# Reading the moving columns of two matrix products in other orders (one-core transformer kernel, Trainium2)

## The chip, the core and the metric

The kernel runs on one core of one Trainium2 chip. The metric is the device time of one execution in microseconds. TensorE has two clock levels, 1.2 and 2.4 GHz; the profile gives the granted clock as a share of the higher one. At 2.4 GHz one column takes 0.4167 ns.

## What is computed

The reference runs two transformer blocks on 256 tokens of width 2048 in fp32. The first is a hybrid of stick-breaking attention and multi-scale pooling, the second retention, a gated delta rule, cross attention and a feed-forward layer. The change touches only the feed-forward layer at the end:

```
h = rms_norm(x, norm_ffn_g)                                # (256, 2048)
x = x + square(relu(h @ w_ff1)) @ w_ff2                    # w_ff1 (2048, 8192), w_ff2 (8192, 2048)
return rms_norm(x, norm_final_g)
```

## The kernel before, in words

**Precision.** Each fp32 operand of a large product is split into a rounded high part and the rest, the low part, both held as fp32r. A product is high times high, plus high times low, plus low times high, summed in PSUM. The matmul takes one operand as stationary weights (128 by 128) and streams the other, the moving operand, past it column by column; each moving column gives one output column in PSUM.

**Weights.** All large weight matrices come in 471 units of up to 2048 columns by 128 partitions. SyncE loads a unit from HBM (`raw`), ScalarE writes the high part (`whi`, line 1704), VectorE subtracts to get the low part (`wlo`, line 2042), each in two halves; `raw`, `whi` and `wlo` have three buffers each. TensorE takes the units in the order of `pairs()`. The order of all engines is written out by hand in `make_plan`, and each engine runs its own steps of that list.

**The feed-forward layer.** It runs in eight blocks of 1024 hidden features. A block b has four products `f1` (256 hidden features each) and then four products `f2` (512 output columns each), each of two units.

- `f1` (kind "T"): the weights are stationary, the activations `AA` moving. `AA` holds the high parts of all activations and, 4352 columns further on, the low parts. For each of 16 pieces of 128 input features and each of 2 output halves there are two matmuls: `whi` against high and low activations together (512 columns, an access of two runs of 256, into one PSUM bank), and `wlo` against the high activations alone (256 columns, into the bank's first half). So a block has 128 matmuls of 512 columns and 128 of 256. VectorE later adds the two halves of the bank (`summed`, line 2065), which reads PSUM with alternating elements 256 columns (1 KB) apart.
- `f2` (kind "N"): the activations `BB` (the block's hidden features) are stationary, the weights moving. For each of 8 pieces and 2 token halves there are three matmuls of 512 columns into one PSUM bank: `whi`, `wlo`, `whi`. So a block has 4 products x 16 x 3 = 192 matmuls of 512 columns. VectorE adds the bank to the residual `XT`.

PSUM has two accumulators of two banks (`double0`, `double1`) that the products use in turn, so reading one out lies beside the next product. Every matmul is issued by `mm_group` (line 1346); all 512 columns of an operand are read in ascending order, `out` in the same order.

**Elsewhere in the kernel**, and of use below: in the gated delta rule the matmuls `g_up` (out `bank`, moving `TT`, stationary `Mn`, 64 columns) read the moving operand by `odd(TT_..., d)`, that is in runs of d columns with d columns left out between them, for d = 2, 4, 8, 16, 32 in this order; `g_down` (moving `Cm`, stationary `Tn`) reads 64 adjacent columns. These are in full fp32, for which the trace has two matmul records each.

Of the kernel before, what the change touches and what calls it, by code (L numbers as in the profile page):

```python
# [13 lines left out]
T = 256  # L14
# [1060 lines left out]
def program(nc, A):  # L1075
# [4 lines left out]
    def S(name):  # L1080
        if name not in sems:
            sems[name] = nc.alloc_semaphore("s_" + name)
        return sems[name]
# [36 lines left out]
    for i in range(4):  # L1120
        o = ar.off
# [139 lines left out]
    def two(x):  # L1261
        return x.rearrange("p (a b) -> p a b", a=2)
# [48 lines left out]
    def hi_of(j):  # L1311
        o = set_off(j)[0]
        return whi[j % SPL][:, o:o + UNIT]

    def lo_of(j):
        o = set_off(j)[1]
        return wlo[j % SPL][:, o:o + UNIT]
# [14 lines left out]
    gdn_end = at["g_tr", 7]["m"]  # L1332


    def tensor_program(q):
        asked = {}

        def free(f):
            if f:
                q.wait_ge(S(f[0]), f[1])  # L1340
# [4 lines left out]
        def mm_group(out, lhsT, rhs, start=True, stop=True):  # L1345
            return q.matmul(out, lhsT, rhs, start=start, stop=stop, skip_group_check=True)  # L1346
# [4 lines left out]
        def operand(pr, a):  # L1351

            if pr["ready"][0] == "b_lo":
                return BB[:, :, a * T:(a + 1) * T]
            if pr["kind"] == "W":
                o, n = a * L, L
            elif pr["tag"] in ("gp", "q", "mp", "ga", "ma"):
                o, n = a * L + META, T
            else:
                o, n = a * T, T  # L1360
            return AA[:, :, o:o + n]

        def mm(key):
            j, half = key
            pi, k, kt, nc_ = units[j]
            pr = P.pairs[pi]
            kind, out = pr["kind"], double[pr["bank"]]
            if k == 0 and half == 0:
                free(pr["freed"])
            if j < 2:  # L1370
                q.wait_ge(S("first_lo"), 2 * j + half + 1)
            else:
                q.wait_ge(S("w_lo"), 2 * j + half + 1)
            split = j in P.split
            if split:
                q.wait_ge(S("w_lo"), 2 * j + 2)
            wh = hi_of(j)[:, 0:kt * nc_].rearrange("p (t c) -> p t c", t=kt)
            wl = lo_of(j)[:, 0:kt * nc_].rearrange("p (t c) -> p t c", t=kt)
            for i in range(kt) if split else range(half * kt // 2, (half + 1) * kt // 2):
                a = k * kt + i  # L1380
                name, ready = pr["ready"]
                if j < 2 and i % 4 == 2:
                    q.wait_ge(S("w_lo"), 2 * j + half + 1)
                if asked.get(name, 0) < ready[a]:
                    asked[name] = ready[a]
                    q.wait_ge(S(name), ready[a])
                both = operand(pr, a)
                hh, hl = both[:, 0, :], both[:, 1, :]
                first, last = k == 0 and i == 0, k == pr["nu"] - 1 and i == kt - 1
                for m in (half,) if split else range(1 if kind == "G" else 2):  # L1390
                    cs = slice(m * 128, (m + 1) * 128)
                    if kind == "W":
                        o = out[:, m * 512:m * 512 + L]
                        mm_group(o, wh[:, i, cs], hh, start=first, stop=False)
                        mm_group(o, wh[:, i, cs], hl, start=False, stop=False)
                        ins = mm_group(o, wl[:, i, cs], hh, start=False, stop=last)
                    elif kind == "N":
                        o = out[:, m * 512:(m + 1) * 512]
                        mm_group(o, hh[:, cs], wh[:, i, :], start=first, stop=False)
                        mm_group(o, hh[:, cs], wl[:, i, :], start=False, stop=False)  # L1400
                        ins = mm_group(o, hl[:, cs], wh[:, i, :], start=False, stop=last)
                    else:
                        n, c = (nc_, slice(0, nc_)) if kind == "G" else (128, cs)
                        mm_group(out[0:n, m * 512:m * 512 + 2 * T], wh[:, i, c], both, start=first, stop=False)
                        ins = mm_group(out[0:n, m * 512:m * 512 + T], wl[:, i, c], hh, start=False, stop=last)
            if split and k:
                ins.then_inc(S("last"), 1)
            elif half == 1:
                ins.then_inc(S("w_used"), 1)
# [276 lines left out]
        for stage, key in P.steps:  # L1686
            if stage == "mm":
                mm(key)
            elif stage in own:
                own[stage](key, at[stage, key])  # L1690
# [1195 lines left out]
    with nc.Block() as block:  # L2886
        @block.tensor
        def _(q):
            tensor_program(q)

        @block.scalar
        def _(q):
            scalar_program(q)

        @block.vector
        def _(q):
            vector_program(q)

        @block.gpsimd
        def _(q):  # L2900
            gpsimd_program(q)

        @block.sync
        def _(q):
            sync_program(q)
# [55 lines left out]
```

## Time and profile before

| | us |
|---|---|
| median of 2 runs | 2870.13 (2869.91 to 2870.35) |
| profiled execution, span from first to last instruction | 2866.7 |
| feed-forward products in the profile | 2187 to 2857 |
| TensorE busy | 2829.8 (99%) |
| VectorE busy | 1931.7 (67%) |
| ScalarE busy | 1355.2 (47%) |

The page has one time for the profiled execution, its span; the runs lie 3.4 us above it. "PE" rows are matmuls, "PEld" rows weight loads, which overlap them. A row of the timeline gives start, duration, and a count if several alike follow each other; the distance between the starts of two matmuls is what one costs in the stream, its duration also holds the way through the array. In names such as `double<-AA,whi` the first input is the moving operand and the second the stationary one.

### The profile page before, as it was taken

How to read it: one execution, taken by the hardware profiler on the slowest of the kernel's cores; microseconds unless marked ns; L12 is line 12 of the kernel's file. 1: busy time of each engine (PE TensorE's matmuls, PEld its weight loads, DVE VectorE, ACT ScalarE, POOL GpSimd, SP SyncE). 2: the span in 40 equal slices, each digit the busy share in tenths (PEclk: the TensorE clock that was granted, in tenths of full speed). 3: DMA queues.
4: the chain of work that ended last, by engine and by line, in shares of the span. 5: the costliest groups of instructions: out<-in, count | busy, mean ns of one | idle time of the engine just before them, and what ended most of it. 6: DMA issues, size and time to landing. Idle time of an engine off the chain costs nothing.

```text
span 2866.7 us, 38752 instructions
## 1 busy us (share of the span) xinstructions
PE 2829.8 (99%) x15872; PEld 2442.7 (85%) x15872; DVE 1931.7 (67%) x2513; ACT 1355.2 (47%) x1729; POOL 57.2 (2%) x102
## 2 busy tenths in 40 slices
PE   9999999999999999999999999999999999999998
PEld 8899888888888888888888888888888888888887
DVE  7645557678766658888888875456666655566556
ACT  5433654357443446555555543444345434444434
POOL 0000210000000000000000000000000000000000
PEclk9999999999999999999999999999999999999999
DMA  7444444564555544334343455544354454554453
GB/s 278 183 184 162 143 166 185 197 231 177 197 184 193 204 151 162 141 139 147 133 145 123 145 175 192 187 182 162 146 200 182 178 204 182 200 200 182 186 196 147
DMA packets 72849, 506.66 MB, mean 177 GB/s; under 512 B 8384, under 2 KB 8512, under 8 KB 12896
## 3 DMA queue, kind: packets, MB, share of 16 engines
q1 hardware_dynamic: 71136, 497.83, 46.9%
q0 software_dynamic: 1104, 5.90, 0.6%
q8 instruction: 126, 2.06, 0.3%
q10 hardware_dynamic: 432, 0.45, 0.0%
q14 instruction: 51, 0.42, 0.0%
HBM read 499.95 MB, written 2.10 MB: 175 GB/s over the span
## 4 chain that ended last, share of the span: by engine, by line
PE 86%; DVE 9%; ACT 3%; issue 2%; DMA 1%; SPq 0%; DVEq 0%; POOL 0%; ACTq 0%
PE double L1346 80%; PE bank L1346 5%; DVE cacc L2048 2%; DVE wlo L2042 2%; ACT whi L1704 1%; DVE cst L2065 1%; PE bank L1349 1%; DVE cacc L2045 1%; ACT L1900 0%; DVE Tn L2556 0%; DVE cst L2042 0%; DVE Cm L2042 0%; ACT tmp L1905 0%; DMA vec<-in_vec 0%; DMA raw<-in_wall 0%
## 5 line engine op out<-in xcount | busy, mean ns | idle before, releaser
L1346 PE MATMUL double<-AA,whi 128*128 128x512 f32 (+1 forms) x5008 | 1643.1, 380 | 3.5 <-DVE wlo L2042 3.3
L1346 PE MATMUL double<-AA,wlo 128*128 128x256 f32 (+1 forms) x4624 | 1297.0, 281 | 0.0
L1704 ACT ACTIVATE whi<-raw 128x1024 fp32r<-128x1024 f32 x926 | 925.2, 1049 | 780.3 <-PE double L1346 748.5
L2042 DVE TENSOR_TENSOR wlo<-raw,whi 128x1024 fp32r<-128x1024 f32 (+1 forms) x934 | 1101.7, 1214 | 229.9 <-ACT whi L1704 227.6
L1346 PEld LDWEIGHTS double<-AA,whi 128*128 128x128 f32 x5008 | 915.9, 188 | 181.2 <-DVE wlo L2042 5.2
L1346 PEld LDWEIGHTS double<-AA,wlo 128*128 128x128 f32 x4624 | 874.7, 189 | 1.5
L1346 PE MATMUL double<-whi,AA 128*128 128x512 f32 x1536 | 487.9, 393 | 0.5 <-DVE wlo L2042 0.5
L1346 PEld LDWEIGHTS double<-whi,AA 128*128 128x128 f32 x1536 | 288.5, 188 | 61.0 <-DVE wlo L2042 1.3
L1346 PE MATMUL double<-whi,BB 128*128 128x512 f32 x1024 | 316.8, 389 | 0.0
L1346 PE MATMUL double<-wlo,AA 128*128 128x512 f32 x768 | 299.1, 389 | 0.0
L1346 PEld LDWEIGHTS double<-whi,BB 128*128 128x128 f32 x1024 | 192.2, 188 | 40.1
L1346 PE MATMUL double<-wlo,BB 128*128 128x512 f32 x512 | 199.3, 389 | 0.0
L1346 PEld LDWEIGHTS double<-wlo,AA 128*128 128x128 f32 x768 | 144.4, 188 | 28.7
L2065 DVE TENSOR_REDUCE tmp<-double 128x512 f32<-128x1024 f32 x60 | 73.4, 1224 | 133.1 <-PE double L1346 133.1
L1346 PEld LDWEIGHTS double<-wlo,BB 128*128 128x128 f32 x512 | 96.1, 188 | 19.8
L2042 DVE TENSOR_TENSOR XT<-double,XT 128x512 f32<-128x512 f32 x64 | 41.3, 686 | 93.0 <-PE double L1346 93.0
L1980 ACT ACTIVATE tmp<-tmp 128x512 f32<-128x512 f32 x32 | 20.2, 633 | 172.1 <-DVE tmp L2048 172.1
L1346 PE MATMUL double<-BB,whi 128*128 128x512 f32 x256 | 90.0, 394 | 0.0
L2048 DVE SCALAR_TENSOR_TENSOR cacc<-cst,vec,cacc 128x256 f32<-128x256 f32 x144 | 69.8, 485 | 5.1
L1346 PE MATMUL double<-BB,wlo 128*128 128x256 f32 x256 | 71.6, 280 | 0.0
L2042 DVE TENSOR_TENSOR X<-double,X 128x512 f32<-128x512 f32 x48 | 33.2, 691 | 53.4 <-PE double L1346 52.5
L2042 DVE TENSOR_TENSOR BB<-tmp,BB 128x512 fp32r<-128x512 f32 x40 | 27.7, 693 | 49.5 <-ACT BB L1753 49.5
(335 smaller groups left out, 1722.2 us busy)
## 6 DMA issues: line engine op xcount, KB each, us to landing
raw<-in_wall SPq DMA_DIRECT2D x462, 1024.0 KB, 4.8
raw<-in_wall SPq DMA_DIRECT2D x9, 256.0 KB, 6.7
X<-in_xT SPq DMA_DIRECT2D x1, 2048.0 KB, 11.4
Mm<-in_memT POOLq DMA_DIRECT2D x1, 2048.0 KB, 15.5
tmp<-rqk POOLq DMA_DIRECT2D x16, 128.0 KB, 2.2
mblk<-in_memT SPq DMA_DIRECT2D x8, 256.0 KB, 4.5
dec<-in_dec POOLq DMA_DIRECT2D x1, 1536.0 KB, 8.6
hs<-in_hsT SPq DMA_DIRECT2D x4, 272.0 KB, 5.2
```

What stands on the lines that cost most here:

```text
L1346: return q.matmul(out, lhsT, rhs, start=start, stop=stop, skip_group_check=True)
L1349: return q.transpose(out, in_, C("ident") if ident is None else ident)
L1704: q.activation(hi_of(j)[:, c], raw[j % RAW][:, c], ACT.Copy).then_inc(S("w_hi"), 1)
L1980: q.activation(x, x, ACT.Square).then_inc(S("f_act"), 1)
L2042: return q.tensor_tensor(out, a, b, o)
L2045: return q.tensor_scalar(out, a, s, None, o)
L2048: return q.scalar_tensor_tensor(out=out, in0=a, scalar=s, in1=b, op0=o0, op1=o1)
L2065: q.reduce_sum(out, both, mybir.AxisListType.X).then_inc(S("sum"), 1)
```

## The change

A table `WAYS` gives thirteen of the sixteen half-blocks another order in which moving columns are read, with the output columns permuted in the same way, so each output column gets what it got before. `("turn", r)` goes in turns between the two halves of the 512 columns, r columns of the one and then r of the other. `("leap", s, r)` reads every s-th chunk of r columns, then the next set, s sets in all. In `f1` a "turn" applies to the 512-column matmuls only (`walk2`), a "leap" to the 256-column ones only (`walk`). In `f2` both apply to all three matmuls. Block 0 of `f1` and blocks 6 and 7 of `f2` stay as they are.

```diff
+    WAYS = {("f1", 1): ("turn", 16), ("f1", 2): ("turn", 4), ("f1", 3): ("turn", 2), ("f1", 4): ("leap", 2, 16), ("f1", 5): ("leap", 4, 16),
+            ("f1", 6): ("leap", 16, 2), ("f1", 7): ("turn", 64),
+            ("f2", 0): ("leap", 2, 16), ("f2", 1): ("leap", 4, 16), ("f2", 2): ("leap", 8, 2), ("f2", 3): ("leap", 2, 8),
+            ("f2", 4): ("turn", 16), ("f2", 5): ("turn", 2)}
...
+        def walk(pr, x):
+
+            way = WAYS.get((pr["tag"], pr["idx"][0])) if pr["tag"] in ("f1", "f2") else None
+            if way is None or way[0] == "turn" and pr["tag"] == "f1":
+                return x
+            if way[0] == "leap":
+                return x.rearrange("p (b s r) -> p s b r", s=way[1], r=way[2])
+            return x.rearrange("p (a b r) -> p b a r", a=2, r=way[1])
+
+        def walk2(pr, x):
+
+            way = WAYS.get((pr["tag"], pr["idx"][0])) if pr["tag"] == "f1" else None
+            if way is None or way[0] == "leap":
+                return x
+            return x.rearrange("p a (b r) -> p b a r", r=way[1])
...
-                        o = out[:, m * 512:(m + 1) * 512]
-                        mm_group(o, hh[:, cs], wh[:, i, :], start=first, stop=False)
-                        mm_group(o, hh[:, cs], wl[:, i, :], start=False, stop=False)
-                        ins = mm_group(o, hl[:, cs], wh[:, i, :], start=False, stop=last)
+                        o, h_, l_ = [walk(pr, x) for x in (out[:, m * 512:(m + 1) * 512], wh[:, i, :], wl[:, i, :])]
+                        mm_group(o, hh[:, cs], h_, start=first, stop=False)
+                        mm_group(o, hh[:, cs], l_, start=False, stop=False)
+                        ins = mm_group(o, hl[:, cs], h_, start=False, stop=last)
...
-                        mm_group(out[0:n, m * 512:m * 512 + 2 * T], wh[:, i, c], both, start=first, stop=False)
-                        ins = mm_group(out[0:n, m * 512:m * 512 + T], wl[:, i, c], hh, start=False, stop=last)
+                        o = out[0:n, m * 512:m * 512 + 2 * T]
+                        if pr["tag"] == "f1" and WAYS.get(("f1", pr["idx"][0]), ("",))[0] == "turn":
+                            mm_group(walk2(pr, two(o)), wh[:, i, c], walk2(pr, both), start=first, stop=False)
+                        else:
+                            mm_group(o, wh[:, i, c], both, start=first, stop=False)
+                        ins = mm_group(walk(pr, o[:, 0:T]), wl[:, i, c], walk(pr, hh), start=False, stop=last)
```

## Rows read from the trace of the kernel before

**Rows 1.** The page: span, busy time of each engine, granted clock by slices.

```profile
span 2866.7 us, 38752 instructions
PE 2829.8 (99%) x15872; PEld 2442.7 (85%) x15872; DVE 1931.7 (67%) x2513; ACT 1355.2 (47%) x1729; POOL 57.2 (2%) x102
PEclk9999999999999999999999999999999999999999
```

**Rows 2.** The chain that ended last, 2180 to 2867 (start us, us, what).

```profile
2187.15 670.27 PE double L1346 x3392
```

**Rows 3.** Who waited for whom, 2190 to 2857 (us in total, times, longest us).

```profile
ACT whi L1704 <- PE double L1346: 200.9, 86, 3.7
DVE XT L2042 <- PE double L1346: 90.4, 32, 3.2
DVE tmp L2065 <- PE double L1346: 79.3, 29, 3.3
```

**Rows 4.** Busy time in two stretches: block 1's f1, then its f2.

```profile
2241.44:2285.81 44.37, 44.37 (x257) 39.23 (x256) 27.38 (x27) 19.55 (x22) 0.00 (x0) 1.00 0.47 179
2285.81:2329.38 43.57, 43.57 (x194) 36.04 (x193) 24.90 (x25) 17.23 (x18) 0.00 (x0) 1.00 0.53 204
```

**Rows 5.** Timeline of TensorE within an f1 product (two runs of 256, then 256).

```profile
2354.91 0.39 PE L1346 MATMUL double<-AA,whi 128*128 128x512 f32 x1
2355.14 0.28 PE L1346 MATMUL double<-AA,wlo 128*128 128x256 f32 x1
...
2357.34 0.39 PE L1346 MATMUL double<-AA,whi 128*128 128x512 f32 x1
```

**Rows 6.** Timeline within an f2 product (512 adjacent columns each).

```profile
2309.66 0.62 PE L1346 MATMUL double<-whi,BB 128*128 128x512 f32 x2
2310.11 0.39 PE L1346 MATMUL double<-wlo,BB 128*128 128x512 f32 x1
...
2312.38 0.39 PE L1346 MATMUL double<-whi,BB 128*128 128x512 f32 x1
```

**Rows 7.** Timeline, one head pair: d = 2, adjacent columns, d = 32.

```profile
1131.69 0.68 PE L1346 MATMUL bank<-TT,Mn 128*64 128x64 f32 x8
1136.18 0.68 PE L1346 MATMUL bank<-Cm,Tn 128*64 128x64 f32 x8
1162.12 0.68 PE L1346 MATMUL bank<-TT,Mn 128*64 128x64 f32 x8
```

**Rows 8.** The chain, 1967 to 1971: full-fp32 matmuls of 256 columns in cross attention.

```profile
1967.07 3.46 PE bank L1346 x16
```

**Rows 9.** All groups of VectorE: two ways of reading PSUM.

```profile
L2065 DVE TENSOR_REDUCE tmp<-double 128x512 f32<-128x1024 f32 x60 | 73.4, 1224 | 133.1 <-PE double L1346 133.1
L2042 DVE TENSOR_TENSOR X<-double,X 128x512 f32<-128x512 f32 x48 | 33.2, 691 | 53.4 <-PE double L1346 52.5
```

## The prediction, made before the kernel was run

> **What bounds the kernel now.** I read the page first. TensorE is busy in 99% of the span, VectorE in 67%, ScalarE in 47%, and all forty slices stand at the higher clock level [rows 1]. Then the chain that ended last: it runs through 3392 matmuls in one piece of 670.27 us, nearly the whole feed-forward layer, which is where all of the change lies; the reader is to see that no other engine's work stands between them [rows 2]. The waits say the same from the other side: ScalarE and VectorE wait for TensorE, up to 3.7 us at a time, and TensorE is in no line of them [rows 3]. In two stretches of one block TensorE is busy all of the time, VectorE for 27.4 of 44.4 us and 24.9 of 43.6 us, and the transfers take half of the DMA engines [rows 4]. So here a nanosecond on a matmul of the stream is a nanosecond on the kernel, up or down: a slower TensorE only makes the others wait more, and a faster one has 16 us a block in hand before VectorE would bind.
>
> Within the stream, a 512-column matmul over adjacent columns costs (2312.38 - 2309.66) / 12 = 226.7 ns [rows 6]. A pair of `f1` costs (2357.34 - 2354.91) / 7 = 347 ns, of which about 230 are the 512 columns in two runs and 117 the 256 columns [rows 5]. As a check, 128 x 347 ns = 44.4 us and 192 x 226.7 ns = 43.5 us, as the two stretches have it [rows 4]. At 2.4 GHz 512 columns are 213.3 ns and 256 are 106.7: the stream goes at one column a cycle and 10 to 17 ns on top of each matmul.
>
> **The change part by part.** It removes and adds no instruction, no wait, no transfer and no byte. Semaphores, buffers, stationary operands and the order of matmuls stay. What changes is how many separate runs an access has. Counted from the table (matmuls x columns / run):
>
> - runs of 2: `f1` block 3, 128 x 512 / 2 = 32,768; `f1` block 6, 128 x 256 / 2 = 16,384; `f2` blocks 2 and 5, 192 x 512 / 2 = 49,152 each. Sum 147,456 runs, 294,912 columns.
> - runs of 4: `f1` block 2, 16,384. Runs of 8: `f2` block 3, 12,288.
> - runs of 16: `f1` block 1, 4,096, blocks 4 and 5, 2,048 each; `f2` blocks 0, 1 and 4, 6,144 each: 26,624. Runs of 64: `f1` block 7, 1,024.
>
> That is 203,776 runs in 2,048 matmuls, where there were 2,560; 201,216 leaps are added. The cost is that number times the price of one leap, twice over: for reading SBUF and for adding into PSUM. Nothing else can cost, since the values and their destinations are the same and whoever reads the bank waits for the last matmul of a product, as before.
>
> **Price of a leap in reading SBUF.** The nearest row is in this kernel. The matmuls of `g_up` read 64 columns in 32 runs of 2 (d = 2), and those of d = 32 in 2 runs of 32; `g_down` reads 64 adjacent columns. All three groups of eight take 0.68 us [rows 7], so 30 leaps more per matmul, 240 in a group, cost under the 10 ns that the row resolves: under 0.04 ns each. The weak point: these are full-fp32 matmuls, of which 256 columns take 3.46 us / 16 = 216 ns [rows 8], so they move at two cycles a column, and a leap that costs up to the spare cycles would not show. The fp32r stream has no spare cycle. The other row is that of `f1`: a matmul of two runs, 17 KB apart, costs 230 ns against 226.7 for one run [rows 5, 6], so one far leap costs 3.3 ns at most, if all of the difference is put down to it. I take zero, because the row of runs of 2 has the very shape of the changed accesses and the other has a different neighbour (a short matmul) that can explain its 3 ns. Ends: 0 and 3.3 ns.
>
> **Price of a leap in PSUM.** No matmul here writes non-adjacent columns. The nearest row is VectorE's read: the sum over the two halves takes 1024 elements from PSUM, each 1 KB from the last, in 1224 ns, and the addition takes 512 in runs of 256 in 691 ns [rows 9]. (1224 - 691) / 512 = 1.04 ns per element and 158 ns fixed in both, so a leap at every element is free at one element per 1.04 ns. TensorE comes to a leap every 0.83 ns in runs of 2 and every 1.67 ns in runs of 4. So runs of 4 or more ask for fewer leaps than PSUM is shown to give free, and only runs of 2 ask for a little more. I take zero again. Bounds: 0 and, in runs of 2, the time of the two columns once more (0.83 ns), unless a leap costs as in the two-run row.
>
> The Trainium skill (SBUF — State Buffer, section "Door 1: The DMA port swizzle") says that SBUF is read in lines of 16 bytes, and that two hits on a line are enough for full speed; runs of two fp32 just meet this, and the row of d = 2 agrees as far as it goes. The Trainium skill (Advanced Engine Details and Errata, section "PSUM Cachelines") speaks against the change: lines are 8 bytes, and "any non-contiguous AP significantly slows down matmuls"; its next sentence softens this, since every two consecutive elements should be contiguous, and here they always are. By the first sentence all thirteen half-blocks would be slower, by the second none; no run so far shows either.
>
> **Sum.** Zero, against the profiled span of 2866.7 us and the runs' 2870.1, which lie 3.4 us above it. Forecast: 2870 us. A change under 57 us (2%) counts as none.
>
> **Rivals.**
>
> *Runs of 2 are at PSUM's limit* (chance 0.12). If a leap can be made only each 1.04 ns, as VectorE's read shows it free, a run of 2 takes 1.04 instead of 0.83 ns: 147,456 x 0.21 = 31 us, 2901 us. Still within 2%. For it: the only rate shown. Against it: that is VectorE's own pace, not a limit.
>
> *Each leap costs TensorE whole cycles; slower* (0.22). Its place is the stream of accumulations in PSUM, or of reads in SBUF. It decides from 57.4 us / 201,216 = 0.29 ns a leap, less than one cycle. If only the runs of 2 pay 0.83 ns, 147,456 x 0.83 = 123 us, 2993 us: block 3 of `f1` would take 32,768 x 0.83 = 27 us longer, and blocks 2 and 5 of `f2` 41 us each. If every leap pays one cycle it is 84 us, 2954 us; if every leap pays two, 168 us, 3038 us. For it: the stream has no idle cycle, and reads by one column a cycle are nowhere shown with short runs. Against it: rows of d = 2 and of VectorE, both at the speed of adjacent columns. The coarse sentence of the Trainium skill named above would be this case.
>
> *A leap costs what the two-run row allows, or more* (0.06): 201,216 x 3.3 ns = 664 us, 3534 us. For it: 230 against 226.7 ns. Against it: at d = 2 the same price would add 30 x 3.3 = 99 ns to a matmul of 64 columns, where nothing is to be seen.
>
> *Faster* (0.08). The 10 to 17 ns on top of each matmul may come from the moving read meeting the next weight load; full-fp32 matmuls of 256 columns have only 2.9 ns of it, 216 against 213.3 [rows 8]. Another order could lessen it. At most 512 x 16.7 + 384 x 10.3 + 1152 x 13.4 ns = 28 us, 2842 us; half of it is 2856 us. It can't reach 2% either.
>
> *The order is lost* (0.02): if the accesses were folded back to adjacent ones, the time would be as before. That is certain for none of the forms, since no two of their runs touch.
>
> **How the numbers follow.** No effect 0.50 (2870), order lost 0.02 (2870), PSUM's limit 0.12 (2901), faster 0.08 (2842 to 2870), whole cycles 0.22 (2954 to 3038), far leap 0.06 (3534). Over 2% faster there is nothing but what I have not thought of, 0.01. Within 2%: 0.50 + 0.02 + 0.12 + 0.08 less that, 0.71. Slower: 0.28. The range from 2855 to 2995 leaves out half of "faster" (0.04), the upper part of "whole cycles" (0.08) and the far leap (0.06), 0.18 in all. The likeliest case's own range is 2867 to 2875.
>
> **What would show each step.** In the changed kernel's trace: the distance of starts in each half-block. 226.7 ns in all of `f2` and 347 ns in all of `f1` confirm the sum, and the chain keeps its one piece of 670 us. If only `f1` 3 and 6 and `f2` 2 and 5 are longer, it is the runs of 2; if `f2` 3 and `f1` 2 are as well, in the ratio of their runs, it is a price per leap. If "turn" and "leap" of one run length differ (`f2` 0 against 4, or 2 against 5), the distance leapt matters. `f1` 6 changes only the 256-column matmuls, whose partner stays as it was, so it gives the price for them alone. Durations of the other rows, the gated delta rule's above all, should not move. The prediction is wrong if the runs of 4 and more cost anything, for then the reasoning by rate fails.

## The result and the profile after

The changed kernel takes 2971.14 us (2969.69 to 2972.59) against 2870.13: a ratio of 1.0357, interval 1.034 to 1.0374, slower by 101 us. I had forecast no change. The profiled execution has a span of 2970.8 us.

The page after. Instructions are as many as before, the clock is at its higher level in every slice, VectorE and ScalarE are busy for the same time to 0.2 us; only TensorE is busy for more time, 104.5 us with matmuls and 20.9 us with weight loads that overlap them [rows 1].

```profile
span 2970.8 us, 38752 instructions
PE 2934.3 (99%) x15872; PEld 2463.6 (83%) x15872; DVE 1931.9 (65%) x2513; ACT 1355.1 (46%) x1729; POOL 57.3 (2%) x102
PEclk9999999999999999999999999999999999999999
```

The chain that ended last, after: the same one piece of 3392 matmuls, 772.99 us instead of 670.27 [rows 2]. It holds 102.7 of the 104.1 us between the two profiled spans.

```profile
2188.55 772.99 PE double L1352 x3392
```

Busy time by half-block (start:end, us, then PE, PEld, DVE, ACT, POOL busy, granted clock, DMA share, GB/s). First `f1` of blocks 1 to 7, then `f2` of blocks 0 to 6. Before, they are 44.37 and 43.57 us; the columns for DVE and ACT are as before to 0.4 us, so neither works more [rows 4].

```profile
2245.57:2291.64 46.07, 46.07 (x257) 39.51 (x256) 27.38 (x27) 19.55 (x22) 0.00 (x0) 1.00 0.47 178
2337.61:2384.54 46.93, 46.93 (x257) 39.26 (x256) 27.38 (x27) 19.87 (x22) 0.00 (x0) 1.00 0.46 177
2467.30:2525.54 58.24, 58.24 (x257) 40.40 (x256) 27.64 (x27) 19.64 (x22) 0.00 (x0) 1.00 0.38 145
2570.16:2616.20 46.04, 46.04 (x257) 39.78 (x256) 27.37 (x27) 19.53 (x22) 0.00 (x0) 1.00 0.45 177
2662.28:2706.66 44.38, 44.38 (x257) 38.85 (x256) 27.37 (x27) 19.53 (x22) 0.00 (x0) 1.00 0.49 181
2770.66:2829.87 59.21, 59.21 (x257) 50.36 (x256) 27.64 (x27) 19.55 (x22) 0.00 (x0) 1.00 0.36 142
2873.42:2917.80 44.38, 44.38 (x258) 39.24 (x257) 27.38 (x27) 19.55 (x22) 0.00 (x0) 1.00 0.48 181
2199.50:2245.57 46.07, 46.07 (x195) 36.20 (x194) 24.90 (x25) 17.22 (x18) 0.00 (x0) 1.00 0.49 188
2291.64:2337.61 45.97, 45.97 (x194) 36.45 (x193) 24.90 (x25) 17.24 (x18) 0.00 (x0) 1.00 0.49 188
2384.54:2467.30 82.76, 82.76 (x194) 39.45 (x193) 24.99 (x25) 17.20 (x18) 0.00 (x0) 1.00 0.27 103
2525.54:2570.16 44.62, 44.62 (x194) 36.10 (x193) 24.90 (x25) 17.24 (x18) 0.00 (x0) 1.00 0.50 189
2616.20:2662.28 46.08, 46.08 (x194) 36.54 (x193) 24.90 (x25) 17.23 (x18) 0.00 (x0) 1.00 0.49 189
2706.66:2770.66 64.00, 64.00 (x195) 37.49 (x193) 24.99 (x25) 17.23 (x18) 0.00 (x0) 1.00 0.36 138
2829.87:2873.42 43.55, 43.55 (x193) 36.07 (x192) 24.90 (x25) 17.23 (x18) 0.00 (x0) 1.00 0.51 193
```

Read as differences from before:

| half-block | order | us more | | half-block | order | us more |
|---|---|---|---|---|---|---|
| f1 1 | turn 16 | 1.7 | | f2 0 | leap (2, 16) | 2.5 |
| f1 2 | turn 4 | 2.6 | | f2 1 | leap (4, 16) | 2.4 |
| f1 3 | turn 2 | 13.9 | | f2 2 | leap (8, 2) | 39.2 |
| f1 4 | leap (2, 16) | 1.7 | | f2 3 | leap (2, 8) | 1.1 |
| f1 5 | leap (4, 16) | 0.0 | | f2 4 | turn 16 | 2.5 |
| f1 6 | leap (16, 2) | 14.8 | | f2 5 | turn 2 | 20.4 |
| f1 7 | turn 64 | 0.0 | | f2 6 | as before | 0.0 |

The four half-blocks with runs of 2 make 88.3 of the 102.7 us; the other 14.4 come from runs of 4 to 16. And one run length has two prices: in `f2`, leaps of 2 cost (82.76 - 43.57) / 192 = 204 ns more a matmul and turns of 2 cost 106 ns more.

### The profile page after: what moved, and what is told of

It is laid out like the page before. It is cut to its first block, busy times and chain, and to the rows that moved or that the text cites. A ratio compares the mean times of both kernels' runs of the same rounds, so it can differ in the third digit from the quotient of the medians.

```text
span 2970.8 us, 38752 instructions
## 1 busy us (share of the span) xinstructions
PE 2934.3 (99%) x15872; PEld 2463.6 (83%) x15872; DVE 1931.9 (65%) x2513; ACT 1355.1 (46%) x1729; POOL 57.3 (2%) x102
## 4 chain that ended last, share of the span: by engine, by line
PE 86%; DVE 8%; ACT 3%; issue 2%; DMA 1%; SPq 0%; DVEq 0%; POOL 0%; ACTq 0%
PE double L1352 81%; PE bank L1352 5%; DVE cacc L2074 2%; DVE wlo L2068 2%; ACT whi L1730 1%; DVE cst L2091 1%; PE bank L1355 1%; DVE cacc L2071 0%; ACT L1926 0%; DVE Tn L2582 0%; DVE cst L2068 0%; DVE Cm L2068 0%; ACT tmp L1931 0%; DMA vec<-in_vec 0%; DMA raw<-in_wall 0%
## 5 line engine op out<-in xcount | busy, mean ns | idle before, releaser
L1352 PE MATMUL double<-AA,whi 128*128 128x512 f32 (+1 forms) x5008 | 1671.1, 384 | 3.3 <-DVE wlo L2068 3.3
L1352 PE MATMUL double<-AA,wlo 128*128 128x256 f32 (+1 forms) x4624 | 1314.5, 284 | 0.0
L1352 PE MATMUL double<-whi,BB 128*128 128x512 f32 x1024 | 363.7, 436 | 0.0
L1352 PE MATMUL double<-wlo,BB 128*128 128x512 f32 x512 | 223.5, 436 | 0.0
L2091 DVE TENSOR_REDUCE tmp<-double 128x512 f32<-128x1024 f32 x60 | 73.4, 1224 | 156.9 <-PE double L1352 156.9
```

Source lines behind the costliest of these rows:

```text
L2091: q.reduce_sum(out, both, mybir.AxisListType.X).then_inc(S("sum"), 1)
```

## The experiments

The sweeps use that the stream has 32 second products (`f2`) of 48 matmuls, each of which can be read in another order within one run: a "slot". A slot's time over 48 is the time of one matmul. With adjacent columns that is 226.7 ns. In the table `SLOTS` a slot has its order, a flag for the order of writes (0: ascending), the number of stationary columns and, from the second sweep on, the shift of the first column.

### Which side pays: reading SBUF or writing PSUM

Two kernels split the change in its two halves. `still` gives an operand the same shape in ascending order. In the first, reads are permuted and writes are not:

```diff
-                        o, h_, l_ = [walk(pr, x) for x in (out[:, m * 512:(m + 1) * 512], wh[:, i, :], wl[:, i, :])]
+                        o, h_, l_ = [f(pr, x) for f, x in ((still, out[:, m * 512:(m + 1) * 512]), (walk, wh[:, i, :]), (walk, wl[:, i, :]))]
```

and the same in `f1`. The second has `walk` on the output and `still` on the two inputs.

> The moving operand is read in the changed orders, the output columns are written in ascending order (so the feed-forward sums land in wrong columns; the work is the same). Theory S, SBUF reading makes the changed half-blocks slow: all of the excess of the changed kernel stays, about +102 us in the feed-forward layer: f2 block 2 (runs of 2, 64 B apart) at 431 ns a matmul, f2 block 5 (runs of 2 in turns) at 333 ns, f1 block 6 +15 us, f1 block 3 +14 us, runs of 16 at 240 ns; 2971 us in all. Theory P, adding into PSUM in leaps makes them slow: nothing is left, 226.7 ns everywhere and 2870 us. Rival: both sides, each in a part of the blocks.

> The mirror image: the moving operand is read in ascending order, the output columns are written in the changed orders (sums land in wrong columns; the work is the same). Theory S: 2870 us and 226.7 ns in all of f2. Theory P: 2971 us and the block times of the changed kernel. If the sides share the cost, the two excesses of a block add up to that of the changed kernel; if the slower side alone sets the pace, the larger of the two is that of the changed kernel.

Reads alone: 2970.98 us, ratio 1.0358 (1.0328 to 1.0388). Writes alone: 2868.25 us, ratio 0.9998 (0.9987 to 1.001). Busy time with reads alone, `f1` 3 and 6, `f2` 2 and 5:

```profile
2466.59:2524.83 58.24, 58.24 (x257) 40.42 (x256) 27.63 (x27) 19.64 (x22) 0.00 (x0) 1.00 0.39 145
2769.95:2829.16 59.21, 59.21 (x258) 50.30 (x256) 27.64 (x27) 19.55 (x22) 0.00 (x0) 1.00 0.38 142
2383.83:2466.59 82.76, 82.76 (x194) 39.41 (x193) 24.98 (x25) 17.20 (x18) 0.00 (x0) 1.00 0.27 104
2705.95:2769.95 64.00, 64.00 (x195) 37.44 (x194) 24.99 (x25) 17.22 (x18) 0.00 (x0) 1.00 0.35 138
```

With writes alone, `f1` 3 and `f2` 2:

```profile
2418.64:2463.01 44.37, 44.37 (x257) 39.22 (x256) 27.37 (x27) 19.55 (x22) 0.00 (x0) 1.00 0.48 181
2375.07:2418.64 43.57, 43.57 (x195) 36.04 (x193) 24.90 (x25) 17.24 (x18) 0.00 (x0) 1.00 0.53 203
```

The first four are those of the changed kernel to a hundredth of a microsecond, the other two those of the kernel before. The whole cost is in reading the moving operand; adding into PSUM in runs of 2 adds nothing, 1 KB apart (`f1` 3) or 64 bytes (`f2` 2). So the sentence of the Trainium skill that any non-contiguous access of PSUM slows a matmul (Advanced Engine Details and Errata, section "PSUM Cachelines") does not hold for any of the thirteen orders here, while its next one, that two consecutive elements should be adjacent, is kept by all thirteen and not put to the test.

### Length of the run or distance of the leap

```diff
+    SLOTS = {
+        (0, 0): (('leap', 2, 2), 0, 128),
+        (0, 1): (('leap', 4, 2), 0, 128),
...
+        (5, 3): (('leap', 2, 1), 0, 128),
+        (6, 0): (('leap', 4, 1), 0, 128),
+        (6, 1): (('leap', 8, 1), 0, 128),
```

> The feed-forward's first products read as before the change. Each of 30 second products (f2, slots (block, j), 48 matmuls of 512 columns each) reads its moving operand in an order of its own and writes in ascending order (sums land in wrong columns; the work is the same): leaps with runs of 2 at steps of 16, 32, 64, 128, 256, 512 and 1024 bytes; runs of 4 at 32 bytes to 1 KB; runs of 8 at 128 bytes to 1 KB; runs of 16 at 512 bytes and 1 KB; runs of 32, 64 and 128; single columns at 8, 16, 32 and 64 bytes; turns of 4, 8 and 32. Theory L (length): the price depends on the length of the run alone, one price per leap: runs of 2 all at 431 ns whatever the step, runs of 4 near 330, of 8 near 275, of 16 near 250. Theory B (place): the price depends on where the next run lies, a leap within 64 bytes being free or nearly so: runs of 2 at a step of 16 or 32 bytes stay well under 431 ns, the step of 64 bytes gives 431 again, and long steps come near the 333 ns of the turns. The changed kernel speaks for B (431 against 333 ns for the same run, 232 ns for runs of 8 and 240 for runs of 16).

One execution, span 2990.8 us. Slots by busy time, in this order: leaps of 2 at steps of 16, 64, 256, 512 and 1024 bytes; leaps of 4 at 64, 128 and 256 bytes; single columns at 8 and 32 bytes.

```profile
2196.45:2218.19 21.74, 21.74 (x50) 9.96 (x49) 7.24 (x7) 5.17 (x6) 0.00 (x0) 1.00 0.29 112
2240.34:2261.05 20.71, 20.71 (x50) 9.89 (x49) 5.92 (x6) 4.01 (x4) 0.00 (x0) 1.00 0.28 102
2327.55:2350.95 23.40, 23.40 (x51) 9.99 (x49) 7.24 (x7) 5.23 (x6) 0.00 (x0) 1.00 0.28 107
2350.95:2372.23 21.28, 21.28 (x49) 9.92 (x48) 5.92 (x6) 4.03 (x4) 0.00 (x0) 1.00 0.27 99
2372.23:2387.99 15.76, 15.76 (x50) 9.38 (x48) 5.92 (x6) 4.01 (x4) 0.00 (x0) 1.00 0.36 133
2443.57:2454.45 10.88, 10.88 (x51) 9.02 (x50) 7.15 (x7) 5.17 (x6) 0.00 (x0) 1.00 0.52 194
2454.45:2466.27 11.82, 11.82 (x49) 9.26 (x48) 5.92 (x6) 4.03 (x4) 0.00 (x0) 1.00 0.58 225
2466.27:2479.62 13.35, 13.35 (x49) 9.27 (x48) 5.92 (x6) 4.23 (x4) 0.00 (x0) 1.00 0.45 157
2750.26:2772.02 21.76, 21.76 (x50) 9.96 (x49) 5.92 (x6) 4.02 (x4) 0.00 (x0) 1.00 0.25 97
2838.53:2859.23 20.70, 20.70 (x49) 9.94 (x48) 5.92 (x6) 4.01 (x4) 0.00 (x0) 1.00 0.27 102
```

The reader is to see three levels. Runs of 2 take 431 to 488 ns (20.71 / 48 = 431) at every step up to 512 bytes, and single columns cost the same as runs of 2: 431 at a step of 32 bytes, where one column of a group of four is wanted, and 453 at a step of 8 bytes, where two of four are wanted one after the other, as with runs of 2 at 16 bytes. So the cost isn't per leap, for with twice the leaps it stays. 431 is 512 columns at two cycles each (426.7) and 5 ns; the 12 to 56 ns more at other steps stay unexplained. Runs of 4 drop to 227 to 278 ns (10.88, 11.82, 13.35 over 48). At 1024 bytes, which is the turn between the two halves, runs of 2 take 328. Both theories fell: L in that runs of 4 do not cost half as much extra as runs of 2 but little or nothing, B in that the near leaps are as dear as the far ones.

### Where a run begins, and the next weight load

Against the sweep before:

```diff
+                        at_ = i * 512 + (0 if e_ == 0 else e_ - 16 * (i % 2))
...
-                        h_, l_ = [walk(x, way, not wr & 2) for x in (wh[:, i, :], wl[:, i, :])]
+                        h_, l_ = [walk(x, way, not wr & 2) for x in (hi_of(j)[:, at_:at_ + 512], lo_of(j)[:, at_:at_ + 512])]
```

> Second products with other variations, reads changed only. Stationary operands of 64 and 32 columns instead of 128 (half and a quarter of the weight load's reads; the rest of the outputs is left out) with adjacent columns, runs of 16, and runs of 2 both ways; starting points shifted by 1, 2, 4 and 8 columns with adjacent columns and with runs of 4, 16 and 2 (wrong columns are summed); writes alone in runs of 2 at 64 bytes. Theory C (contention): the 13 ns on top of each adjacent matmul, and the further 13 ns with runs of 16, are reads of the next weight load taking turns with the moving read: with 32 stationary columns adjacent reads fall from 226.7 to about 217 ns and runs of 16 from 240 to about 220. Rival: they belong to the moving read alone and stay at 226.7 and 240. Runs of 2 stay at 431 and 333 ns under both, less some 13 under C. A shifted start costs nothing if lines of 16 bytes do not matter; if they do, runs of 4 shifted by 1 or 2 columns touch twice as many lines and get slower, those shifted by 8 do not. Writes alone: 226.7 ns.

One execution, span 2937.5 us. First, 32 stationary columns with adjacent reads and with runs of 16; then runs of 4 at steps of 128 bytes, shifted by 1, 2 and 8 columns.

```profile
2211.40:2222.53 11.13, 11.13 (x50) 5.26 (x48) 5.92 (x6) 4.02 (x4) 0.00 (x0) 1.00 0.59 227
2234.04:2245.56 11.52, 11.52 (x50) 5.30 (x48) 5.92 (x6) 4.01 (x4) 0.00 (x0) 1.00 0.47 182
2498.47:2519.24 20.77, 20.77 (x51) 9.95 (x49) 7.24 (x7) 5.16 (x6) 0.00 (x0) 1.00 0.32 124
2519.24:2540.50 21.26, 21.26 (x50) 9.95 (x48) 5.92 (x6) 4.01 (x4) 0.00 (x0) 1.00 0.26 99
2540.50:2552.42 11.92, 11.92 (x49) 9.22 (x48) 5.92 (x6) 4.02 (x4) 0.00 (x0) 1.00 0.48 176
```

A shift by 1 or 2 columns takes runs of 4 from 246 to 433 and 443 ns, a shift by 8 to 248: what counts is whether a run is a whole aligned group of four columns, 16 bytes. Adjacent columns shifted by 1, 2, 4 or 8 take 233 to 237, so it isn't the start alone. The contention theory in its stated form fell: with a quarter of the weight columns the adjacent reads take 232 ns and not less than 226.7, and runs of 16 stay at 240. Leaps of 2 at 64 bytes, which it had at 431 or a little less, even took 22.82 / 48 = 475 ns with 32 stationary columns (430 with 64), which no theory here explains. A part that a weight load costs whatever its size is not excluded.

### Are half-read lines paid by the column?

A fourth sweep made this quantitative: runs of 8, 16, 32 and 64 shifted by 2 columns, so that each run has two half lines at its ends.

```diff
+    SLOTS = {
+        (0, 0): (('leap', 2, 8), 0, 128, 2),
+        (0, 1): (('leap', 2, 16), 0, 128, 2),
+        (0, 2): (('leap', 2, 32), 0, 128, 2),
+        (0, 3): (('leap', 2, 64), 0, 128, 2),
...
+        (2, 3): (('turn', 1), 0, 128, 0),
+        (3, 0): (('turn', 2), 0, 128, 1),
+        (3, 1): (('turn', 4), 0, 128, 2),
```

> One slot of 48 matmuls each, second products, reads in leaps that begin 1, 2 or 4 columns off a line of 16 bytes (wrong columns are summed), writes in ascending order. Theory W (whole lines): a column costs one cycle when all four columns of its line are read together, and two when the line is read in part. Then runs of 8 shifted by 2 are 2 + 4 + 2 columns, half of them double: 1.5 x 213 + some 15 = 335 ns; runs of 16: 1.25 x 213 + 15 = 282; of 32: 255; of 64: 241; the same for a shift by 1 but for the split. A shift by 4 columns costs nothing: runs of 8 232, of 16 240, of 4 about 224 to 246. Runs of 4 shifted by 2: 440. Turns of 4 shifted by 2: as turns of 2 where the other line is kept, about 330, if the keeping holds. Turns of single columns: about 330 or more. Rival, a price for each run that does not begin on a line: runs of 8 as dear as runs of 4 are per run, (440 - 227) / 128 = 1.7 ns, so 334, 280, 253: the same, unless the shift by 1 differs from that by 2. Leap (4, 8) and (4, 4), reads alone and with writes, tell whether the 220 ns seen with reads alone is real: 220 against 230.

One execution, span 2905.7 us. Runs of 8, 16, 32 and 64, shifted by 2; runs of 8 shifted by 4; turns of a single column.

```profile
2196.80:2212.68 15.88, 15.88 (x50) 9.36 (x49) 7.24 (x7) 5.16 (x6) 0.00 (x0) 1.00 0.40 154
2212.68:2226.32 13.64, 13.64 (x49) 9.27 (x48) 5.92 (x6) 4.02 (x4) 0.00 (x0) 1.00 0.41 154
2226.32:2238.87 12.55, 12.55 (x49) 9.25 (x48) 5.92 (x6) 4.01 (x4) 0.00 (x0) 1.00 0.44 168
2238.87:2250.99 12.12, 12.12 (x50) 9.10 (x49) 5.92 (x6) 4.02 (x4) 0.00 (x0) 1.00 0.48 173
2324.78:2335.90 11.12, 11.12 (x49) 9.03 (x48) 5.92 (x6) 4.01 (x4) 0.00 (x0) 1.00 0.49 189
2435.70:2446.06 10.36, 10.36 (x49) 9.07 (x48) 5.92 (x6) 4.02 (x4) 0.00 (x0) 1.00 0.52 203
```

331, 284, 261 and 252 ns, where 335, 282, 255 and 241 were expected; 232 for the shift by 4. Theory W stands within 11 ns; a shift by 1 gives 330 and 283 for runs of 8 and 16, the same as by 2. Its rival, a price per unaligned run, gives the same numbers here, so this sweep alone does not part them; single columns at the price of runs of 2, in the length sweep, speak against any price per run. The last row is a surprise: turns of single columns take 216 ns, 11 less than adjacent reading, where I expected 330 or more. The slots for leap (4, 8) gave 230.7 both ways and (4, 4) 226.5, so the 220 ns that (4, 8) had in one slot of the length sweep was not found again.

### What turns gain: returning to a line

```diff
+            if way[0] == "turn256":
+                return x[:, 0:256].rearrange("p (a b r) -> p b a r", a=2, r=way[1])
+            if way[0] == "apart":
+                return x.rearrange("p (a b s r) -> p s b a r", a=2, s=2, r=way[1])[:, 0]
+            if way[0] == "short":
+                return x[:, 0:256]
```

> Whole runs of 4 columns or more in other orders, and three tests of what the turns of 2 gain. Second products, one slot each: turns of 2 between two quarters 512 bytes apart, 256 columns a matmul; the same turns, 1 KB apart, but only every other pair, so that no line of 16 bytes is come back to; 256 adjacent columns; both turns with runs of 4 (in these five slots half the output columns are left out); then leaps in runs of 8 to 64. Theory R (return): a line left half read is kept over one other run, so turns of 2 cost half of what leaps of 2 cost: the turns 512 bytes apart take about 165 ns for 256 columns, those without return about 215. Theory D (distance): 1 KB apart is cheaper than near, whatever is returned to: 215 for 512 bytes, 165 without return. Adjacent: 117 to 120. Leaps (4, 8): 220 again against 226.7 adjacent, for the steps place the reads and the next weight load differently; if that was chance the slots scatter from 220 to 240 for no rule. First products: 28 combinations of orders for the 512 and for the 256 columns; adjacent 347 ns a pair, and if (4, 8) is a gain there too, 340 or less.

One execution, span 2860.9 us. Turns of 2 at 512 bytes, turns of 2 at 1 KB without return, 256 adjacent columns:

```profile
2200.24:2208.40 8.16, 8.16 (x50) 8.16 (x49) 6.45 (x7) 5.12 (x6) 0.00 (x0) 1.00 0.29 97
2208.40:2220.44 12.04, 12.04 (x50) 10.15 (x49) 6.61 (x7) 4.16 (x4) 0.00 (x0) 1.00 0.78 311
2220.44:2226.22 5.78, 5.78 (x50) 5.77 (x49) 5.49 (x6) 4.02 (x4) 0.00 (x0) 1.00 0.32 113
```

170, 251 and 120 ns, where theory R had 165 and 215 for the first two and theory D the reverse. At one distance, 1 KB, 256 columns take 164 ns with the return (half of the 328 above) and 251 without: the turns of 2 are cheaper than the leaps because the other half of the line is wanted after one other run, not because it is far. The 36 ns above 215 stay open. Of the 29 combinations in `f1`, none was better than 346.0 ns a pair against 347 adjacent; turns of 4, 8 and 32 columns in the 512-column matmul cost 6 to 20 ns.

The last sweep took single columns in turns from 2, 4, 8 or 16 streams.

```diff
+            if way[0] == "weave":
+                return x.rearrange("p (o c b) -> p o b c" if order else "p (o b c) -> p o b c", c=way[1], b=way[2])
```

> Second products, one slot each, single columns read in turns from 2, 4, 8 or 16 streams whose starts lie 2 to 256 columns apart (reads alone; wrong columns are summed). Theory R (a line half read is kept over one other): two streams are fast at every distance, about 216 ns, from 4 columns (the next line) to 256; two streams 2 columns apart stay in one line and are as adjacent, 216 to 227; with four or more streams the line is gone before its next column is wanted, 431 ns or more, as with leaps of single columns. Theory D (distance matters, not the return): only 128 and 256 columns apart are fast. If four streams are fast too, more than two lines are kept.

One execution, span 2911.8 us. Two streams 2, 4 and 16 columns apart, then four streams 4 apart, eight streams 4 apart.

```profile
2197.76:2208.68 10.92, 10.92 (x50) 9.01 (x49) 7.15 (x7) 5.18 (x6) 0.00 (x0) 1.00 0.46 175
2208.68:2219.04 10.36, 10.36 (x49) 9.07 (x48) 5.92 (x6) 4.01 (x4) 0.00 (x0) 1.00 0.65 251
2229.40:2239.76 10.36, 10.36 (x49) 9.07 (x48) 5.92 (x6) 4.02 (x4) 0.00 (x0) 1.00 0.52 202
2369.96:2382.85 12.89, 12.89 (x50) 9.13 (x49) 7.24 (x7) 5.17 (x6) 0.00 (x0) 1.00 0.54 212
2467.34:2490.36 23.02, 23.02 (x51) 10.01 (x49) 7.24 (x7) 5.17 (x6) 0.00 (x0) 1.00 0.28 109
```

Two streams take 215.8 ns at every distance from 4 to 256 columns, 227 within one line. Four streams 4 or more columns apart take 269 to 283, not the 431 that "kept over one other" would give; eight take 480 to 489, sixteen 435. Four streams 2 apart, which is two columns of one line and then two of the next in turns, take 340, near the 328 of turns of 2. So theory R is right for two lines and too strict for four: it looks as if more than one other line is kept, and fewer than seven. That a line is "kept" is a reading of these times and not shown, and it doesn't say why two streams of single columns are faster than turns of 2 (328) and even than adjacent reading.

### Undoing and resizing the change

Two kernels tested the sum. One leaves the four half-blocks with runs of 2 as they were before the change, the other makes them runs of 4. The table of the second, against the changed kernel:

```diff
-    WAYS = {("f1", 1): ("turn", 16), ("f1", 2): ("turn", 4), ("f1", 3): ("turn", 2), ("f1", 4): ("leap", 2, 16), ("f1", 5): ("leap", 4, 16),
-            ("f1", 6): ("leap", 16, 2), ("f1", 7): ("turn", 64),
-            ("f2", 0): ("leap", 2, 16), ("f2", 1): ("leap", 4, 16), ("f2", 2): ("leap", 8, 2), ("f2", 3): ("leap", 2, 8),
-            ("f2", 4): ("turn", 16), ("f2", 5): ("turn", 2)}
+    WAYS = {("f1", 1): ("turn", 16), ("f1", 2): ("turn", 4), ("f1", 3): ("turn", 4), ("f1", 4): ("leap", 2, 16), ("f1", 5): ("leap", 4, 16),
+            ("f1", 6): ("leap", 16, 4), ("f1", 7): ("turn", 64),
+            ("f2", 0): ("leap", 2, 16), ("f2", 1): ("leap", 4, 16), ("f2", 2): ("leap", 8, 4), ("f2", 3): ("leap", 2, 8),
+            ("f2", 4): ("turn", 16), ("f2", 5): ("turn", 4)}
```

> The change without its four half-blocks of runs of 2 (f1 blocks 3 and 6, f2 blocks 2 and 5). From the block times of the changed kernel the rest is worth +1.7, +2.6, +1.7 and 0 in f1 and +2.5, +2.4, +1.0 and +2.5 in f2: 14 us over the kernel before, 2884 us. If the half-blocks influenced each other or the clock, it would come out elsewhere. My own forecast of the price by rate would have had 2870.

Measured: 2883.22 us, ratio 1.0052 (1.0035 to 1.0068).

> The changed kernel with one size changed: its four half-blocks of runs of 2 get runs of 4 (turns of 4; leaps (16, 4) in f1 block 6 and (8, 4) in f2 block 2). Theory W: every line is read whole, so nearly all of the cost goes. By the slots of the sweeps f2 block 2 costs 246 ns a matmul (+3.8 us), f2 block 5 250 ns (+4.5), f1 block 3 as block 2 (+2.6), f1 block 6 a pair of 367 ns (+2.5); with the 14 us of the rest 2897 us. A theory of a price per leap that falls by half with half as many leaps would give 2928.

Measured: 2896.97 us, ratio 1.0101 (1.0085 to 1.0116). Both came out within 1 us of the number, so half-blocks add up and the runs of 2 are 88 us of the loss. With half the leaps in those four the price fell from 88 us to 14 (2896.97 - 2883.22), not to 44.

### Two versions that read in another order on purpose

```diff
+    WAY_N = ("leap", 4, 4)
...
+                        o, h_, l_ = [walk(x, way) for x in (out[:, m * 512:(m + 1) * 512], wh[:, i, :], wl[:, i, :])]
```

> The kernel before with all its 3,840 matmuls of kind N (512 moving weight columns) reading and writing in leaps (4, 4), runs of one whole line at steps of 64 bytes, the fastest order met that keeps the sums in place: 223.5 against 226.7 ns in one slot. 3,840 x 3.2 ns = 12 us: 2857 us, a ratio of 0.996. If the slot's 3 ns depended on where its buffers lay, the ratio is 1.000.

Measured: 2863.95 us, ratio 0.9985 (0.9976 to 0.9994): a gain of 0.15%, 4.7 of the 12 us that the slot promised. In the profile its `f2` matmuls start 226.5 ns apart, as (4, 4) did in two of three sweeps; the 3 ns of the third weren't found again.

The other uses the two streams. Reads are woven, outputs stand interleaved in PSUM, and whoever reads them takes them apart:

```diff
+    def woven(x, n=2):
+        return x.rearrange("p (c b) -> p b c", c=n)
...
+                        o, h_, l_ = out[:, m * 512:(m + 1) * 512], woven(wh[:, i, :]), woven(wl[:, i, :])
...
+                        if kind == "T":
+                            b_, h_ = both.rearrange("p a (c b) -> p a b c", c=2), woven(hh)
...
-            both = double[r["b"]][:, :].rearrange("p (m x t) -> p m t x", m=2, x=2)
-            q.reduce_sum(out, both, mybir.AxisListType.X).then_inc(S("sum"), 1)
+            both = double[r["b"]][:, :].rearrange("p (m x b c) -> p m c b x", m=2, x=2, c=2)
+            q.reduce_sum(out.rearrange("p m (c b) -> p m c b", c=2), both, mybir.AxisListType.X).then_inc(S("sum"), 1)
```

> A version made from one slot of the partial-line sweep: turns of a single column between two halves 1 KB apart took 216 ns for 512 columns, 10.7 ns less than adjacent reading. Here all matmuls of the kinds N (3,840) and T (4,480 pairs) of the whole kernel read that way (N between halves of 512, T between halves of 256 columns, 512 bytes apart), the outputs are written in ascending order, so interleaved, and VectorE and ScalarE take the columns apart where they read PSUM; the result is the reference's. If both kinds get 216 ns per 512 and about 109 per 256 columns: 3,840 x 10.7 = 41 us and 4,480 x 22 = 99 us off, 2729 us. If pairs of T are held at 347 ns by something else (the weight loads), only the 41 us: 2828 us. If reading PSUM interleaved costs VectorE more than its 1.04 ns per element, its evictions grow but TensorE still hides them. Rival: the 216 ns was an accident of the slot's buffers: 2869 us.

Measured: 2753.87 us, ratio 0.9601 (0.9588 to 0.9614), 4.0% faster than the kernel before and 7.3% faster than the changed one. Page, the piece of the chain that holds the feed-forward layer (670.27 us before), block 1's `f1` and `f2`, and the two groups of VectorE:

```profile
span 2749.6 us, 38752 instructions
PE 2699.5 (98%) x15872; PEld 2426.0 (88%) x15872; DVE 1930.8 (70%) x2513; ACT 1352.7 (49%) x1729; POOL 56.8 (2%) x102
...
2104.81 635.46 PE double L1354 x3392
...
2156.57:2198.49 41.92, 41.92 (x257) 38.52 (x256) 27.38 (x27) 19.51 (x22) 0.00 (x0) 1.00 0.50 186
2198.49:2239.93 41.44, 41.44 (x194) 36.29 (x193) 24.90 (x25) 17.23 (x18) 0.00 (x0) 1.00 0.57 219
...
L2075 DVE TENSOR_REDUCE tmp<-double 128x512 f32<-128x1024 f32 x60 | 73.5, 1224 | 105.7 <-PE double L1354 105.7
L2052 DVE TENSOR_TENSOR X<-double,X 128x512 f32<-128x512 f32 x48 | 33.1, 690 | 44.1 <-PE double L1354 43.3
```

A pair of `f1` takes 41.92 / 128 = 327.5 ns instead of 346.6, a matmul of `f2` 215.8 instead of 226.7. Reading PSUM interleaved costs VectorE nothing (1224 and 690 ns, as in [rows 9]). 3,840 x 10.9 + 4,480 x 19.1 ns = 127 us were to be had by these rows, 115 came. The profile has the rest as waits: TensorE is busy for 130.3 us less, but idle for 50.1 us (2749.6 - 2699.5) instead of 36.9, and as it has no gap in the feed-forward layer, these 13 us lie before it, where the other engines hold it up. My 2729 us had left that out.

## Why the prediction was wrong

**What bounds the kernel: right.** The chain kept its one piece, and what the stream lost the kernel lost (102.7 us in the chain, 101 in the time). One reading beside it was off: by [rows 4] VectorE has 17 to 19 us in hand in each half-block, not 16 in a block; nothing hung on it.

**The counting: right.** Thirteen half-blocks, no other work touched.

**The price of a leap in PSUM, zero: right**, and shown by the kernel with writes alone, 0.9998. But the argument for it was weak, and that it came right is luck: two rows were solved for two unknowns, the fixed part and the rate, so they could not show that a leap at every element is free, and VectorE's rate would still have allowed a cost for runs of 2 (the 31 us rival). There was none.

**The price of a leap in reading SBUF, zero: the step that failed.** I took it from the matmuls of the gated delta rule, because their runs of 2 had "the very shape of the changed accesses" [rows 7]. I had written beside it that they move at two cycles a column [rows 8], and two cycles a column is just what half-read lines cost. The row could not show the price, and so was no evidence for zero. The shape was the wrong thing to match; the rate was the right one. A row that has slack where the changed code has none only bounds what it may hide, here one more cycle a column, and that bound I should have put on the runs of 2: 294,912 columns x 0.417 ns = 123 us. What the runs showed in place of zero: 431 instead of 226.7 ns a matmul in leaps of 2, 88.3 us for the four half-blocks of runs of 2, and 14.4 us for the runs of 4 to 16. The 2971 us lie within my range of 2855 to 2995 only because its upper part stood for the rival of whole cycles, not by my own sum.

**The unit of the price** was wrong as well. I reckoned in leaps. What counts is whether whole groups of 16 bytes are read: runs of 4 that fill such groups pay little at any number of leaps, and single columns, with twice the leaps, pay no more than runs of 2.

**The rivals.** "Each leap costs TensorE whole cycles", at 0.22, was the case nearest to what came, in its first form, only runs of 2 pay: 123 us against 88.3 measured, beside 14.4 for longer runs that this form left free. It put `f1` 3 at 27 us and `f2` 2 and 5 at 41 each; they were 13.9, 39.2 and 20.4. The leap (8, 2) was as priced, the two turns at half of it, because the line is returned to. The others did not come: PSUM showed no limit, no leap costs 3.3 ns, the orders were not lost, and nothing in this change was faster, though the room for it, 10 to 17 ns on top of each matmul, was real and another order took most of it. The sign that I had named, full-fp32 matmuls with only 2.9 ns on top, was good; the guess that the next weight load causes the rest is not borne out, since a quarter of its columns left it in place, but how it comes about stays open.

**What would have shown it wrong** was that runs of 4 or more cost anything. They did, 14.4 us.

**The Trainium skill**, SBUF — State Buffer, section "Door 1: The DMA port swizzle": the line of 16 bytes is what the runs show, to the shift of one column. That two hits on a line are enough for full speed they do not show: at one cycle a column two hits take 431 ns, as one does, and only whole lines (220 to 278 ns) or a return after one other column (216) come near full speed or reach it. The measurement decides.

## What to carry to other kernels

Where TensorE bounds the kernel, stream the moving fp32r operand in whole aligned groups of four columns (16 bytes), and where there is a choice, weave two streams column by column: that took 11 ns off each matmul of 512 and 4% off this kernel, since interleaved outputs cost nothing to take apart in PSUM (VectorE 1224 and 690 ns, as before). Permute outputs in PSUM freely, at least in runs of two. And before a row is taken as evidence that something is free, compare its rate with that of the changed code: an operation that runs at half speed can hide whatever costs up to the other half.

## What had not been expected of the hardware

- Single columns from two streams are read faster than adjacent ones: 215.8 against 226.7 ns for 512 columns, at all distances from 16 bytes to 1 KB.
- A column of a half-read 16-byte line costs two cycles whether one or two columns of the line are wanted (431 ns both). The times look as if a line stays at hand over one other (turns of 2, 328 ns), partly over three (four streams, 269 to 283), not over seven (480); that is a reading, not shown.
- Left open: why whole lines at some steps cost 20 to 50 ns more (runs of 4 at 256 bytes 278, at 512 bytes 268, in turns 250), why runs of 16 stand at 240 in three different orders (and at 231 in a fourth, leap (8, 16)) while runs of 8 in leap (2, 8) have 232 and runs of 64 have 227, why two streams beat adjacent reading, and what the last 13 ns on top of an adjacent matmul are. Fewer weight columns did not lessen them; the order of reading did.
